# Moving the transposes that close the SSD branch's gated norm into the following weight unit

## The chip, the cores and the metric

The kernel runs on one core of a Trainium2 chip, as one launch. The metric is device time in microseconds, median over several executions. A second number is the time of the one execution that the hardware profiler recorded; all rows below are from that execution.

## The reference, cut to what matters

A decoder trunk of two layers over 256 tokens, width 1024, float32. In each layer one projection feeds three mixers (sliding-window attention A, block attention B, a Mamba-2 SSD branch C), whose outputs are gated and merged; cross-attention and an MLP follow. The part that the change touches is the end of branch C and what reads it:

```python
y = ssd_scan(xh, dt, a, bm, cm) + xh * d_skip[:, None]
y = y.reshape(B, S, SSD_D_INNER) * silu(z)
yg = y.reshape(B, S, SSD_GROUPS, SSD_D_INNER // SSD_GROUPS)        # 2 groups of 512 columns
yg = yg * rsqrt(mean(yg * yg, axis=-1, keepdims=True) + NORM_EPS)
y_c = yg.reshape(B, S, SSD_D_INNER) * ssd_norm
...
merged = g_a * (y_a @ w_br_swa) + g_b * (y_b @ w_br_moba) + g_c * (y_c @ w_br_ssd)
```

## The kernel before, in words

**Weight units.** All dense products of a layer are cut into 93 units, `UNITS[0]` to `UNITS[92]`, each with 1 MB of weights or less, in a ring of three buffers (`RING = 3`). For each unit SyncE's queue (SP) issues the load into `raw` (L606), ScalarE (ACT) rounds it to `w_hi` (`hi`, L721), VectorE (DVE) makes the remainder `w_lo` (`lo`, L1344), and TensorE (PE) multiplies: three products for each tile pair (hi by hi, hi by lo, lo by hi; L1041 to L1043), 48 matmuls of 256 columns in each unit that matters here. Every engine walks the same list of units, written out by hand, in program order; what an engine does in its turn for unit `u` is called slot `u`. In slot `u` ACT and DVE prepare unit `u + 3`, since that buffer is free once unit `u` is done. So in ACT's slot `u` stand, in this order: the closing work of the slot, the evacuation of unit `u`, `hi(u + 3)`, and the exponentials of a job. DVE's slot: the mask of a job, the closing work, the evacuation, `lo(u + 3)`.

**Units around the change.** 27 to 30 are gate columns of branch B, 31 and 32 are `branch_b` (y_b times its weights), 33 to 36 gate columns of branch C, 37 to 40 `branch_c` (y_c times `w_br_ssd`), 41 to 44 the mixing product.

**Small work between units.** Attention and SSD work is placed behind units: 24 jobs (numbers 16 to 23 are the SSD's, at slots 25 to 32), each with a mask on DVE (L1573), an exponential on ACT (L834), a weighting on GpSimd (POOL, L670), and "values" on PE two slots later (`job_values`, eight small matmuls, L1147). SP's queue carries a broadcast of 256 KB for each SSD job (L591) ahead of a weight load; that of job 23 and behind it the load of unit 34 wait for the mask of job 21 (`decays_made`), made in slot 30.

**Closings.** `CLOSINGS` 4 to 7 are the four blocks (128 tokens by 512 columns) of branch C. Closing `i` is at slot `CLOSE_SLOT[i]`: 28, 30, 32, 34. There DVE makes `y_tok` (`close`, L1630 and L1632), ACT squares it with a sum (`close_square`, L858), POOL turns the sum to a reciprocal root in three small operations (L693 to L696), and ACT scales `y_tok` (`close_scale`, L851), at the head of ACT's next slot. Then PE transposes the block (`close_turn`, four 128 by 128 transposes, L1168, into the PSUM bank 7), ACT copies the result times a gain as `yc_hi` (`close_hi_part`, L873, four operations), and DVE makes the remainder `yc_lo` and frees the bank (`close_lo_part`, L1647, four operations). For closings 6 and 7, PE first computes a term "yoff" (two passes at L1233, right behind units 32 and 34) into the same bank 7, so that it waits for the release of that bank. Unit 37 waits for the release of closing 7's bank (`operand_ready`): only then y_c is complete.

**Before the change** all three steps of closing `i` are in slot `CLOSE_SLOT[i] + 1`: PE transposes behind units 29, 31, 33 and 35 (and behind the values of that slot).

Of the kernel before, what the change touches and what calls it, by code (L numbers as in the profile page):

```python
# [134 lines left out]
UNITS = make_units()  # L135
# [12 lines left out]
U_GATE, U_BRA, U_BRB, U_BRC, U_MIX = (first_of(k) for k in ("gate", "branch_a", "branch_b", "branch_c", "mix"))  # L148
# [8 lines left out]
def job_slot(n):  # L157

    return JOB_SLOT0 + n + (SSD_PAUSE if n >= SSD_JOB0 else 0)


def job_at(s):

    return next((n for n in range(NJOBS) if job_slot(n) == s), -1)
# [19 lines left out]
def head_of(j, i):  # L184
# [6 lines left out]
CLOSINGS = [(3, 0, 0, 0), (7, 0, 1, 0), (11, 1, 0, 0), (15, 1, 1, 0),  # L191
            (17, 2, 0, 0), (19, 2, 0, 1), (21, 2, 1, 0), (23, 2, 1, 1)]
CLOSE_SLOT = [job_slot(c[0]) + 2 for c in CLOSINGS]


SB_, TB_, OB_, YB_ = 4, 5, 6, 7
# [11 lines left out]
def slot_banks(s):  # L208

    out = []  # L210
    if s == SWA_T_SLOT:
        out += [(b, ("qkT", i)) for i, b in enumerate((SB_, TB_, OB_))]
    if 0 <= job_at(s) < SSD_JOB0:
        out.append((SB_, ("score", job_at(s))))
    if 0 <= job_at(s - 1) < SSD_JOB0:
        out.append((TB_, ("probsT", job_at(s - 1))))
    if job_at(s - 2) in [0, 4, 8, 12, 16, 18, 20, 22]:
        out.append((OB_, ("values", job_at(s - 2))))
    if s == ACS_SLOT:
        out.append((YB_, ("acs",)))  # L220
    if s == CB_SLOT:
        out.append((YB_, ("cb",)))
    if s == BTOK_SLOT:
        out.append((YB_, ("btok",)))
    if s in XS_SLOTS:
        out += [(YB_, ("xs", XS_SLOTS.index(s), 0)), (SB_, ("xs", XS_SLOTS.index(s), 1))]
    if s == STATES_SLOT:
        out += [(YB_, ("states", 0)), (SB_, ("states", 1))]
    for i, (_, branch, tile, group) in enumerate(CLOSINGS):
        if branch == 2 and tile == 1 and s == CLOSE_SLOT[i]:  # L230
            out.append((YB_, ("yoff", group)))
    for i in range(8):
        if s == CLOSE_SLOT[i] + 1:
            out.append((YB_, ("closeT", i)))
    for n in (1, 2):
        if s == NORM_TURN_SLOT[n]:
            out += [(SB_ + b, ("norm", n, b)) for b in range(4)]
    if s in (U_CO + 2, U_CO + 3):
        out += [(SB_ + b, ("norm", 3, b)) for b in ((0, 1), (2, 3))[s - U_CO - 2]]
    h = s - CROSS_SLOT0  # L240
    if 0 <= h < X_HEADS:
        out.append((SB_, ("xscore", h)))
    if 0 <= h - 1 < X_HEADS:
        out.append((TB_, ("xprobsT", h - 1)))
    if s == U_VX + 2:
        out += [(OB_, ("xvalues", 0)), (YB_, ("xvalues", 1))]
    if s == U_VX + 3:
        out += [(OB_, ("xvalues", 2)), (YB_, ("xvalues", 3))]
    return out
# [58 lines left out]
def trunk(nc, a, out):  # L308
    ctx = ExitStack()
    with ctx:  # L310
# [173 lines left out]
        def bank(key):  # L484
            return psum[:, BANK_OF[key][0], :]
# [223 lines left out]
        def _(act):  # L709
# [186 lines left out]
            for l in range(DEPTH):  # L896
# [20 lines left out]
                for u, w in enumerate(UNITS):  # L917
                    h = u - CROSS_SLOT0
                    for i in range(4, 8):
                        if u == CLOSE_SLOT[i] + 1:  # L920
                            close_scale(l, i)
                    if u == SWA_T_SLOT:
                        for i in range(3):
                            act.wait_ge(*is_full(l, ("qkT", i)))
                            out_of_bank(l, ("qkT", i), qkT_a[:, 2 * i:2 * i + 2, :], two(bank(("qkT", i))))
                    turned_probs(l, job_at(u - 1))
                    if u == CB_SLOT:
                        act.wait_ge(*is_full(l, ("cb",)))
                        out_of_bank(l, ("cb",), cbT[:].rearrange("p k n -> p (k n)"))
                    if u == BTOK_SLOT:  # L930
                        act.wait_ge(*is_full(l, ("btok",)))
                        out_of_bank(l, ("btok",), b_tok[:].rearrange("p k n -> p (k n)"), bank(("btok",))[:, 0:SEQ])
                    if u == STATES_SLOT:
                        for g in range(SSD_GROUPS):
                            act.wait_ge(*is_full(l, ("states", g)))
                            out_of_bank(l, ("states", g), states[:, g, :])
                    for i in range(8):
                        if u == CLOSE_SLOT[i] + 1:
                            close_hi_part(l, i)
                    if 0 <= h - 1 < X_HEADS:  # L940
                        act.wait_ge(*is_full(l, ("xprobsT", h - 1)))
                        out_of_bank(l, ("xprobsT", h - 1), pT_x[:, h - 1, :, :], two(bank(("xprobsT", h - 1))))
                    if w["kind"] == "xbc":
                        hi(l, u + RING)
                    if u in (U_CO + 2, U_CO + 3):
                        norm_gain_hi(l, 3, ((0, 1), (2, 3))[u - U_CO - 2])
                    evacuate(l, u)
                    if w["kind"] == "branch_c":
                        merged_hi(l, w["index"])
                    if u + RING < NU and w["kind"] != "xbc":  # L950
                        hi(l, u + RING)
                    if u == U_SWA:
                        act.wait_ge(*sp_arg.at(l, 1))
                        act.activation(sp[:, 1, :], sp[:, 0, :], ACT.Exp, scale=-1.0).then_inc(sp_exp.sem, 1)
                        act.activation(par[:, PC_EXPA:PC_DSKIP], cols[:, l, PC_EXPA:PC_DSKIP], ACT.Exp)\
                           .then_inc(a_exp.sem, 1)
                    if u == ACS_SLOT:
                        act.wait_ge(*decay_arg.at(l, 1))
                        act.activation(decay[:], decay[:], ACT.Exp).then_inc(decay_exp.sem, 1)
                    for i in range(4, 8):  # L960
                        if u == CLOSE_SLOT[i]:
                            close_square(l, i)
                    exps(l, job_at(u))
                    if 0 <= h < X_HEADS:
                        cross_exps(l, h)
                    for hh in {U_VX + 2: (0, 1), U_VX + 3: (2, 3)}.get(u, ()):
                        cross_out_hi(l, hh)
                    if u == MEM_SQUARE_SLOT:
                        act.wait_ge(*mem_loaded.at(l, 16))
                        act.wait_ge(*ssd_sq.at(l, 4))  # L970
                        for t in range(TT):
                            square(1, t, mem_sb, sq_done.sem)
                    for n in (1, 2):
                        if u == NORM_TURN_SLOT[n]:
                            norm_gain_hi(l, n)
                    if u == NORM_TURN_SLOT[2] or u == U_CO + 3:
                        for t in range(TT):
                            square(2 if u < U_CO else 3, t, x_sb, sq_done.sem)
# [5 lines left out]
        def _(pe):  # L984
# [30 lines left out]
            def unit(l, u, tiles=range(TT)):  # L1015
# [18 lines left out]
                if w["orient"] == "A":  # L1034
                    for m in range(n // P):
                        dst = bank(unit_banks(u, w)[m // 2])[:, (m % 2) * SEQ:(m % 2 + 1) * SEQ]
                        for k in range(kt):
                            if turned and m == 0 and k % 2 == 0:
                                pe.wait_ge(*is_read(l, ("norm", turned, k // 2)))
                            cs = slice(m * P, (m + 1) * P)  # L1040
                            pe.matmul(dst, m_hi[:, k, cs], a_hi[:, k, :], start=k == 0, stop=False)  # L1041
                            pe.matmul(dst, m_hi[:, k, cs], a_lo[:, k, :], start=False, stop=False)  # L1042
                            ins = pe.matmul(dst, m_lo[:, k, cs], a_hi[:, k, :], start=False, stop=k == kt - 1)  # L1043
# [160 lines left out]
            for l in range(DEPTH):  # L1204
                for u in range(NU):
# [43 lines left out]
                    if u == CB_SLOT:  # L1249
                        pe.wait_ge(*xbc_ready.at(l, 6))  # L1250
                        pe.wait_ge(*is_free(l, ("cb",)))
                        for c in range(TT):
                            for g in range(SSD_GROUPS):
                                i = SSD_GROUPS * c + g
# [24 lines left out]
                            pe.matmul(bank(key), b_tok[:, g, :], xdec[:, 512 * g:512 * (g + 1)],  # L1279
                                      start=True, stop=True).then_inc(full(key), 1)  # L1280
                    for i in range(8):
                        if u == CLOSE_SLOT[i] + 1:
                            close_turn(l, i)
                    if 0 <= h < X_HEADS:
                        cross_scores(l, h)
# [9 lines left out]
        def _(dve):  # L1295
# [382 lines left out]
            for l in range(DEPTH):  # L1678
# [7 lines left out]
                lo(l, 2)  # L1686
                for u, w in enumerate(UNITS):
                    h = u - CROSS_SLOT0
                    if 0 <= job_at(u):
                        job_mask(l, job_at(u))  # L1690
                    if u == ACS_SLOT:
# [3 lines left out]
                    if u in XS_SLOTS:  # L1695
                        xs_tokens(l, XS_SLOTS.index(u))
                    for i in range(8):
                        if u == CLOSE_SLOT[i] + 1:
                            close_lo_part(l, i)
                    for i in range(8):  # L1700
                        if u == CLOSE_SLOT[i]:
# [21 lines left out]
                    if 0 <= h < X_HEADS:  # L1723
                        dve.wait_ge(*is_read(l, ("xscore", h)))
                        steps.link(dve.reciprocal(row_max[:], xden[:]))
                        for t in range(TT):
                            s = s_sb[:, h % 2, t * SEQ:(t + 1) * SEQ]
# [43 lines left out]
```

## Time and profile before

| | us |
|---|---|
| median of 3 runs | 1233.14 (1230.57 to 1234.44) |
| profiled execution, its own time | 1229.25 |
| its span, first to last instruction | 1227.5 |
| PE busy | 1183.4 |
| DVE busy | 741.4 |
| ACT busy | 587.4 |
| POOL busy | 87.3 |

The engines' busy times overlap. In the page and the rows, "L1168" is line 1168 of the kernel; `PEld` is the loading of the stationary operand, which overlaps with matmuls. The mean granted clock of TensorE over the execution is 0.997 of full speed. The core's DMA engines move 163 GB/s on average.

### The profile page before, as it was taken

How to read it: one execution, taken by the hardware profiler on the slowest of the kernel's cores; microseconds unless marked ns; L12 is line 12 of the kernel's file. 1: busy time of each engine (PE TensorE's matmuls, PEld its weight loads, DVE VectorE, ACT ScalarE, POOL GpSimd, SP SyncE). 2: the span in 40 equal slices, each digit the busy share in tenths (PEclk: the TensorE clock that was granted, in tenths of full speed). 3: DMA queues.
4: the chain of work that ended last, by engine and by line, in shares of the span. 5: the costliest groups of instructions: out<-in, count | busy, mean ns of one | idle time of the engine just before them, and what ended most of it. 6: DMA issues, size and time to landing. Idle time of an engine off the chain costs nothing.

```text
span 1227.5 us, 19222 instructions
## 1 busy us (share of the span) xinstructions
PE 1183.4 (96%) x8014; PEld 1085.5 (88%) x8014; DVE 741.4 (60%) x1080; ACT 587.4 (48%) x800; POOL 87.3 (7%) x119
## 2 busy tenths in 40 slices
PE   2999999999999999999989999999999999999997
PEld 1998899999898899999879888999999978999996
DVE  3776766685745465555458767568675544645554
ACT  4544544545454354444445554445554444544442
POOL 4000001420000000000020000023100000000000
PEclk9999999999999999999999999999999999999999
DMA  6652534547654446555627444266556453555561
GB/s 154 202 167 75 181 123 140 174 150 258 192 167 133 144 158 200 183 196 171 206 84 228 137 138 135 81 180 217 179 180 198 138 171 104 205 187 191 182 211 38
DMA packets 155424, 201.37 MB, mean 164 GB/s; under 512 B 6097, under 2 KB 110921, under 8 KB 155337
## 3 DMA queue, kind: packets, MB, share of 16 engines
q1 hardware_dynamic: 155208, 200.08, 50.1%
q8 instruction: 64, 1.05, 0.4%
q0 software_dynamic: 128, 0.06, 0.3%
q14 instruction: 24, 0.19, 0.1%
HBM read 199.04 MB, written 1.08 MB: 163 GB/s over the span
## 4 chain that ended last, share of the span: by engine, by line
PE 87%; DVE 4%; ACT 3%; issue 2%; POOL 2%; DMA 2%; SPq 1%; DVEq 0%; POOLq 0%; ACTq 0%
PE psum L1041 15%; PE psum L1042 15%; PE psum L1043 15%; PE psum L1050 10%; PE psum L1052 10%; PE psum L1051 10%; PE psum L1114 2%; PE psum L1155 2%; PE psum L1127 1%; PE psum L1200 1%; PE psum L1177 1%; DMA raw<-in_w_br_moba_dram 1%; PE psum L1085 1%; POOL sms L693 1%; DVE w_lo L1344 1%
## 5 line engine op out<-in xcount | busy, mean ns | idle before, releaser
L1344 DVE TENSOR_TENSOR w_lo<-raw,w_hi 128x2048 fp32r<-128x2048 f32 (+1 forms) x184 | 418.7, 2278 | 267.4 <-ACT w_hi L721 267.4
L721 ACT ACTIVATE w_hi<-raw 128x2048 fp32r<-128x2048 f32 (+2 forms) x188 | 349.2, 1858 | 153.6 <-PE psum L1052 130.9
L1041 PE MATMUL psum<-act_hi,w_hi 128*128 128x256 f32 x1344 | 385.3, 287 | 0.0
L1043 PE MATMUL psum<-act_hi,w_lo 128*128 128x256 f32 x1344 | 380.1, 283 | 0.0
L1042 PE MATMUL psum<-act_lo,w_hi 128*128 128x256 f32 x1344 | 380.1, 283 | 0.0
L1041 PEld LDWEIGHTS psum<-act_hi,w_hi 128*128 128x128 f32 x1344 | 257.6, 192 | 1.9 <-issue 0.5
L1042 PEld LDWEIGHTS psum<-act_lo,w_hi 128*128 128x128 f32 x1344 | 257.7, 192 | 1.1 <-issue 0.5
L1043 PEld LDWEIGHTS psum<-act_hi,w_lo 128*128 128x128 f32 x1344 | 257.5, 192 | 0.0
L1050 PE MATMUL psum<-w_hi,relu_hi 128*128 128x512 f32 x256 | 99.8, 390 | 0.0
L1051 PE MATMUL psum<-w_lo,relu_hi 128*128 128x512 f32 x256 | 99.8, 390 | 0.0
L1052 PE MATMUL psum<-w_hi,relu_lo 128*128 128x512 f32 x256 | 99.6, 389 | 0.0
L1050 PE MATMUL psum<-w_hi,act_hi 128*128 128x512 f32 (+1 forms) x224 | 87.2, 389 | 4.4 <-issue 4.4
L1051 PE MATMUL psum<-w_lo,act_hi 128*128 128x512 f32 (+1 forms) x224 | 85.2, 380 | 0.0
L1052 PE MATMUL psum<-w_hi,act_lo 128*128 128x512 f32 (+1 forms) x224 | 85.2, 380 | 0.0
L777 ACT ACTIVATE tmp<-psum 128x512 f32<-128x512 f32 x32 | 19.1, 597 | 96.0 <-PE psum L1043 96.0
L756 ACT ACTIVATE pT_sb<-psum 128x256 f32<-128x256 f32 (+1 forms) x32 | 15.7, 490 | 96.1 <-PE psum L1127 96.1
L658 POOL TENSOR_TENSOR ms<-sq,pool_c 128x1 f32<-128x1 f32 (+1 forms) x12 | 9.1, 759 | 693.9 <-ACT tmp L728 642.4
L1052 PEld LDWEIGHTS psum<-w_hi,relu_lo 128*128 128x128 f32 x256 | 48.1, 188 | 10.1
L1050 PEld LDWEIGHTS psum<-w_hi,relu_hi 128*128 128x128 f32 x256 | 48.1, 188 | 9.5
L1051 PEld LDWEIGHTS psum<-w_lo,relu_hi 128*128 128x128 f32 x256 | 48.1, 188 | 9.5
L1050 PEld LDWEIGHTS psum<-w_hi,act_hi 128*128 128x128 f32 x224 | 42.8, 191 | 12.5 <-issue 5.4
L1052 PEld LDWEIGHTS psum<-w_hi,act_lo 128*128 128x128 f32 x224 | 42.8, 191 | 8.2
(245 smaller groups left out, 1788.9 us busy)
## 6 DMA issues: line engine op xcount, KB each, us to landing
raw<-in_w_in_dram SPq DMA_DIRECT2D x36, 1024.0 KB, 5.2
raw<-in_w_up_dram SPq DMA_DIRECT2D x32, 1024.0 KB, 5.4
raw<-in_w_down_dram SPq DMA_DIRECT2D x32, 1024.0 KB, 5.1
raw<-in_w_gate_dram SPq DMA_DIRECT2D x24, 1024.0 KB, 7.1
raw<-in_w_ckv_dram SPq DMA_DIRECT2D x16, 1024.0 KB, 5.3
raw<-in_w_br_ssd_dram SPq DMA_DIRECT2D x8, 1024.0 KB, 9.6
raw<-in_w_mix_out_dram SPq DMA_DIRECT2D x8, 1024.0 KB, 5.1
raw<-in_w_cq_dram SPq DMA_DIRECT2D x8, 1024.0 KB, 5.1
```

The costliest lines, as they stand in the source:

```text
L721: ins = act.activation(w_hi[:, slot, cut], raw[:, slot, cut], ACT.Copy)
L756: act.activation(dst, src, ACT.Copy).then_inc(free(key), 1)
L777: act.activation(tmp[:, j % 2, :], bank((u, 0)), ACT.Relu).then_inc(free((u, 0)), 1)
L1041: pe.matmul(dst, m_hi[:, k, cs], a_hi[:, k, :], start=k == 0, stop=False)
L1042: pe.matmul(dst, m_hi[:, k, cs], a_lo[:, k, :], start=False, stop=False)
L1043: ins = pe.matmul(dst, m_lo[:, k, cs], a_hi[:, k, :], start=False, stop=k == kt - 1)
L1050: pe.matmul(dst, a_hi[:, k0 + k, ts], m_hi[:, k, :], start=first, stop=False)
L1051: pe.matmul(dst, a_hi[:, k0 + k, ts], m_lo[:, k, :], start=False, stop=False)
L1052: ins = pe.matmul(dst, a_lo[:, k0 + k, ts], m_hi[:, k, :], start=False, stop=last)
L1114: ins = pe.matmul(bank(key)[:, i * 2 * P:i * 2 * P + (t + 1) * P], qk[half_p, q_tile, t * P:(t + 1) * P], qk[half_p, k_tile, 0:(t + 1) * P ...
L1155: ins = pe.matmul(bank(key)[:, hs], pT_sb[:, n % 2, c:c + P], v, start=k == 0, stop=k == t)
L1344: dve.tensor_tensor(w_lo[:, slot, 0:n], raw[:, slot, 0:n], w_hi[:, slot, 0:n].bitcast(F32), ALU.subtract).then_inc(lo_ready.sem, 1)
```

## The change

The transposes of closings 4 to 7 move one slot on, into the inside of a unit. For closings 0 to 3 nothing changes. `INNER_TURN` is {30: (4, (1, 0)), 32: (5, (1, 0)), 34: (6, (1, 0)), 36: (7, (0, 4))}: inside unit 30, closing 4's transposes stand ahead of column tile m = 1, inner tile k = 0, and so on. Units 30, 34 and 36 have two column tiles of eight inner tiles, so (1, 0) is behind 24 of the 48 matmuls and (0, 4) behind 12; unit 32 has four column tiles of four inner tiles, so (1, 0) is behind 12. ACT's `close_hi_part` and DVE's `close_lo_part` move on to slots 30, 32, 34 and 36 too, and DVE's stands at the head of its slot, ahead of the mask. `close_scale`, `close_square` and `close` stay. In bank 7 the order of use stays closing 5, yoff, closing 6, yoff, closing 7.

```diff
--- before.py
+++ after.py
@@ -191,6 +191,9 @@
 CLOSINGS = [(3, 0, 0, 0), (7, 0, 1, 0), (11, 1, 0, 0), (15, 1, 1, 0),
             (17, 2, 0, 0), (19, 2, 0, 1), (21, 2, 1, 0), (23, 2, 1, 1)]
 CLOSE_SLOT = [job_slot(c[0]) + 2 for c in CLOSINGS]
+TURN_SLOT = [CLOSE_SLOT[i] + (1 if c[1] < 2 else 2) for i, c in enumerate(CLOSINGS)]
+INNER_TURN = {TURN_SLOT[i]: (i, (0, 4) if i == 7 else (1, 0)) for i, c in enumerate(CLOSINGS) if c[1] == 2}
+assert all(UNITS[u]["orient"] == "A" and u < U_BRC for u in INNER_TURN)
 
 
 SB_, TB_, OB_, YB_ = 4, 5, 6, 7
@@ -226,12 +229,12 @@
         out += [(YB_, ("xs", XS_SLOTS.index(s), 0)), (SB_, ("xs", XS_SLOTS.index(s), 1))]
     if s == STATES_SLOT:
         out += [(YB_, ("states", 0)), (SB_, ("states", 1))]
+    for i in range(8):
+        if s == TURN_SLOT[i]:
+            out.append((YB_, ("closeT", i)))
     for i, (_, branch, tile, group) in enumerate(CLOSINGS):
         if branch == 2 and tile == 1 and s == CLOSE_SLOT[i]:
             out.append((YB_, ("yoff", group)))
-    for i in range(8):
-        if s == CLOSE_SLOT[i] + 1:
-            out.append((YB_, ("closeT", i)))
     for n in (1, 2):
         if s == NORM_TURN_SLOT[n]:
             out += [(SB_ + b, ("norm", n, b)) for b in range(4)]
@@ -935,7 +938,7 @@
                             act.wait_ge(*is_full(l, ("states", g)))
                             out_of_bank(l, ("states", g), states[:, g, :])
                     for i in range(8):
-                        if u == CLOSE_SLOT[i] + 1:
+                        if u == TURN_SLOT[i]:
                             close_hi_part(l, i)
                     if 0 <= h - 1 < X_HEADS:
                         act.wait_ge(*is_full(l, ("xprobsT", h - 1)))
@@ -1035,6 +1038,8 @@
                     for m in range(n // P):
                         dst = bank(unit_banks(u, w)[m // 2])[:, (m % 2) * SEQ:(m % 2 + 1) * SEQ]
                         for k in range(kt):
+                            if u in INNER_TURN and INNER_TURN[u][1] == (m, k):
+                                close_turn(l, INNER_TURN[u][0])
                             if turned and m == 0 and k % 2 == 0:
                                 pe.wait_ge(*is_read(l, ("norm", turned, k // 2)))
                             cs = slice(m * P, (m + 1) * P)
@@ -1279,7 +1284,7 @@
                             pe.matmul(bank(key), b_tok[:, g, :], xdec[:, 512 * g:512 * (g + 1)],
                                       start=True, stop=True).then_inc(full(key), 1)
                     for i in range(8):
-                        if u == CLOSE_SLOT[i] + 1:
+                        if u == TURN_SLOT[i] and u not in INNER_TURN:
                             close_turn(l, i)
                     if 0 <= h < X_HEADS:
                         cross_scores(l, h)
@@ -1686,6 +1691,8 @@
                 lo(l, 2)
                 for u, w in enumerate(UNITS):
                     h = u - CROSS_SLOT0
+                    if u in INNER_TURN:
+                        close_lo_part(l, INNER_TURN[u][0])
                     if 0 <= job_at(u):
                         job_mask(l, job_at(u))
                     if u == ACS_SLOT:
@@ -1695,7 +1702,7 @@
                     if u in XS_SLOTS:
                         xs_tokens(l, XS_SLOTS.index(u))
                     for i in range(8):
-                        if u == CLOSE_SLOT[i] + 1:
+                        if u == TURN_SLOT[i] and u not in INNER_TURN:
                             close_lo_part(l, i)
                     for i in range(8):
                         if u == CLOSE_SLOT[i]:
```

## Rows read from the trace of the kernel before

**Rows 1.** Page, part 4: shares of the span on the chain that ended last.
```profile
PE 87%; DVE 4%; ACT 3%; issue 2%; POOL 2%; DMA 2%; SPq 1%; DVEq 0%; POOLq 0%; ACTq 0%
```

**Rows 2.** Waits of PE: line, releaser, us in total, times, longest.
```profile
PE psum L1168 <- ACT y_tok L851: 5.1, 7, 1.3
```

**Rows 3.** Timeline of PE, layer 0: start, duration, line, operands, count [idle before].
```profile
231.10 1.00 PE L1147 MATMUL psum<-xdt,s_sb 128*128 128x64 f32 x8
232.95 0.66 PE L1168 MATMUL psum<-ident,y_tok 128*128 128x128 f32 x4 [0.85 <-ACT y_tok L851]
233.36 0.36 PE L1041 MATMUL psum<-act_hi,w_hi 128*128 128x256 f32 x1
...
245.84 1.00 PE L1147 MATMUL psum<-xdt,s_sb 128*128 128x64 f32 x8
247.00 0.66 PE L1168 MATMUL psum<-ident,y_tok 128*128 128x128 f32 x4 [0.15 <-ACT y_tok L851]
...
253.24 1.02 PE L1233 MATMUL psum<-states,xbcT 128*128 128x512 f32 x2
254.10 1.00 PE L1147 MATMUL psum<-xdt,s_sb 128*128 128x64 f32 x8
254.91 0.36 PE L1041 MATMUL psum<-act_hi,w_hi 128*128 128x256 f32 x1
...
260.74 1.00 PE L1147 MATMUL psum<-xdt,s_sb 128*128 128x64 f32 x8
262.83 0.66 PE L1168 MATMUL psum<-ident,y_tok 128*128 128x128 f32 x4 [1.09 <-ACT y_tok L851]
...
276.45 0.28 PE L1043 MATMUL psum<-act_hi,w_lo 128*128 128x256 f32 x1
277.03 0.66 PE L1168 MATMUL psum<-ident,y_tok 128*128 128x128 f32 x4 [0.30 <-ACT y_tok L851]
...
283.27 0.28 PE L1041 MATMUL psum<-yc_hi,w_hi 128*128 128x256 f32 x1
```

**Rows 4.** Timeline of PE, layer 1: closing 4.
```profile
832.52 0.66 PE L1168 MATMUL psum<-ident,y_tok 128*128 128x128 f32 x4 [1.29 <-ACT y_tok L851]
```

**Rows 5.** Timeline of ACT, layer 0: `hi(34)`, closing 7's `yc_hi`, `hi(38)`.
```profile
249.59 1.92 ACT L721 ACTIVATE w_hi<-raw 128x2048 fp32r<-128x2048 f32 x1 [0.76 <-DMA raw<-in_w_gate_dram]
...
277.72 1.14 ACT L873 ACTIVATE yc_hi<-psum,par 128x128 fp32r<-128x128 f32 x4 [0.75 <-PE psum L1168]
...
281.11 1.91 ACT L721 ACTIVATE w_hi<-raw 128x2048 fp32r<-128x2048 f32 x1 [1.51 <-DMA raw<-in_w_br_ssd_dram]
```

**Rows 6.** Timeline of DVE, layer 0: masks 21 and 23, an evacuation, `lo(35)`, `yc_lo`, `lo(38)`.
```profile
240.31 1.41 DVE L1573 SCALAR_TENSOR_TENSOR s_sb<-pT_sb,acs,mask_ssd 128x128 f32<-128x128 f32 x4 [0.67 <-PE psum L1147]
...
255.84 1.13 DVE L1573 SCALAR_TENSOR_TENSOR s_sb<-pT_sb,acs,mask_ssd 128x128 f32<-128x128 f32 x4
...
261.00 0.68 DVE L1526 SCALAR_TENSOR_TENSOR tmp<-g_sb,psum 128x512 f32<-128x512 f32 x1
...
262.32 3.36 DVE L1344 TENSOR_TENSOR w_lo<-raw,w_hi 128x2048 fp32r<-128x2048 f32 x1
...
278.90 1.13 DVE L1647 SCALAR_TENSOR_TENSOR yc_lo<-psum,par,yc_hi 128x128 fp32r<-128x128 f32 x4 [3.62 <-ACT yc_hi L873]
283.05 2.29 DVE L1344 TENSOR_TENSOR w_lo<-raw,w_hi 128x2048 fp32r<-128x2048 f32 x1 [3.02 <-ACT w_hi L721]
```

**Rows 7.** Timeline of POOL, layer 0: a small operation of closing 6, weighting of job 23.
```profile
261.21 0.19 POOL L694 TENSOR_TENSOR sms<-sms,pool_c 128x1 f32<-128x1 f32 x1
...
261.99 1.54 POOL L670 TENSOR_TENSOR s_sb<-s_sb,cbT 128x512 f32<-128x512 f32 x1
```

**Rows 8.** Timeline of SP's queue, layer 0: broadcast for job 23, load 34 behind it.
```profile
241.74 0.34 SPq L591 DMA_DIRECT2D pT_sb<-acs_rows  x1
```

**Rows 9.** Timeline of PE at the layers' border, and its clock there.
```profile
624.52 0.47 PE L1050 MATMUL psum<-w_hi,act_hi 128*128 128x512 f32 x1 [2.78 <-issue]
```

**Rows 10.** Windows: length, busy us of PE, PEld, DVE, ACT, POOL, granted clock, DMA.
```profile
625.40:628.40 3.00, 3.00 (x9) 2.32 (x8) 2.48 (x3) 0.16 (x2) 2.61 (x3) 0.50 0.20 68
```

## The prediction

> **What bounds the kernel now.** I read the chain of waits first: PE holds 87% of it, DVE, ACT and POOL together 9% [rows 1]. So time comes and goes where PE stands still. The table of PE's waits says for what: at the closings' transposes it waits 5.1 us in 7 pieces for ACT's scaled `y_tok` [rows 2]. PE has no wait between the last of them in a layer and the end of `branch_c`, so whatever is lost or won at the closings goes straight to the end. Third, the timelines of PE, ACT, DVE, POOL and SP side by side through one layer's closings: there one sees what is ready when the transposes come half a unit later.
>
> **What is removed.** Eight values take 0.81 us up to the next instruction (254.10 to 254.91 in [rows 3]). PE would be free for the transposes at 231.91, 246.65, 261.55 and, one matmul of 0.12 behind 276.45, at 276.57; they start at 232.95, 247.00, 262.83 and 277.03 [rows 3]. That is 1.04 + 0.35 + 1.28 + 0.46 = 3.13 us in layer 0. In layer 1 the idle time before closing 4 is 1.29 instead of 0.85 [rows 3, 4], so 3.57. Inside a unit the four transposes still take 0.41 (232.95 to 233.36), and the first matmul behind them is 0.36 long instead of 0.28 [rows 3]: one more such switch than before, 0.09 each, 0.36 in a layer. If nothing else waited, the gain would be 2.8 + 3.2 = 6.0 us. The new places are late enough for `y_tok`: by the same rows (its transposes started as soon as it was there) it is ready just before 232.95, 247.00 and 262.83, and PE would come by at 231.91 + 0.08 + 24 x 0.12 = 234.9, about 247.2 and about 264.5. Only closing 5 is tight (0.1 to 0.4 us).
>
> **What is moved, and what stands ahead of it.** `yc_hi` and `yc_lo` now stand in the next slot of ACT and DVE, so behind `hi(u)` and `lo(u)` of a unit three ahead of the slot they left: closing 4 behind hi and lo of unit 32, closing 5 of unit 34, closing 6 of 36, closing 7 of 38. In each of these slots the weights must have landed before the closing can be read. Someone waits for that reading: nobody for closing 4; for closing 5 and 6 the yoff pass behind units 32 and 34 (same bank); for closing 7 unit 37.
>
> *Closing 4.* Its transposes are over at 235.4, ACT and DVE read it by about 239.2. DVE's mask 21 waits for the values behind unit 30 anyway, which come at 238.25 instead of 239.20; a mask starts 1.11 behind them (240.31 - 239.20). So mask 21 is not delayed, and 0.95 us of the gain is kept up to here. It ends at 240.5 instead of 241.7: the start is earlier by 0.95 and it is 1.14 long instead of 1.41, since POOL has finished. SP waits for it with the broadcast of job 23 and load 34 [rows 8], so these go out 1.2 us earlier.
>
> *Closing 5.* `hi(34)` starts when load 34 lands, at 249.59 [rows 5]; 1.2 earlier is 248.4. It takes 1.95 to DVE's start (281.11 to 283.05 for unit 38 [rows 5, 6]), so `lo(34)` runs from 250.35 for 2.2 (2.29, of which the next instruction overlaps 0.1), and `yc_lo` from 252.6 for 1.13 [rows 6]: bank 7 is free at 253.75. PE wants it for yoff at 246.65 - 0.95 + 0.08 + 5.76 + 0.5 = 252.05. So yoff starts at about 253.8 instead of 253.24 [rows 3]: the lead of 1.2 us that PE had has become a lag of 0.56. Both ends: if load 34 lands no earlier, because the transfer and not its issue sets it, 1.2 more; if it lands early enough for `lo(34)` to be done by 251, nothing is lost (lag -1.2). POOL's weighting of job 22 runs just then. `lo(35)` beside the weighting of job 23 took 3.36 instead of 2.29 [rows 6, 7]; if `yc_lo` were held up the same way, 1.1 more. I take none: POOL's L694 ran at 261.21 for 0.19 inside DVE's L1526, which reads PSUM and one tile of SBUF as `yc_lo` does [rows 6, 7]. The Trainium skill ("SBUF — State Buffer", Who interferes with whom) says that a DVE instruction with two SBUF inputs locks out a GpSimd one that reads SBUF and the reverse, whichever is first, and one with a single SBUF input does not; the trace agrees on both, 3.36 beside 2.29 and 0.19 undisturbed. By the rule applied to `lo(34)`, which starts before that weighting, POOL waits and not DVE.
>
> *Closing 6.* Mask 23 was held by DVE itself (255.84 [rows 6]); now it waits for values 21, 0.86 + 1.11 behind yoff: 255.8, the same. `lo(35)` ends at 265.6, `lo(36)` follows until 267.8, `yc_lo` until 268.85, while PE, 0.56 late, wants yoff at 261.55 + 0.56 + 5.84 (the unit) + 0.5 (the transposes) = 268.45. A stall of 0.5; the lag falls from 0.56 to about -0.1.
>
> *Closing 7.* Here is the largest term. SP holds load 38 behind the memory's load, and that behind the last `y_tok` (closing 7), so `hi(38)` waits for DMA and starts at 281.11 [rows 5], and `lo(38)` at 283.05 [rows 6]. Both move with PE's lag only (-0.1). Before, `yc_hi` (277.72) and `yc_lo` (278.90) ran in the 3 us in which ACT and DVE were waiting for this load. Now `yc_hi` comes at 282.9 and `yc_lo` behind `lo(38)`: 282.95 + 2.2 = 285.2, plus 1.13, plus 0.1 to PE: unit 37 starts at 286.4. PE would have been ready at 276.57 - 0.1 + 0.08 + 5.76 + 0.5 = 282.8. It stands 3.6 us still, and unit 37 starts 3.15 later than at 283.27 [rows 3]. Layer 1 is the same with numbers 0.2 to 0.4 smaller (mask 21 gains 1.65 instead of 1.2): about +2.9. Nothing gives it back: units 37 to 44 are PE bound, and their loads are ahead.
>
> **The clock.** A pause of 2.78 us at the layers' border is followed, some 0.8 us after PE's restart, by 3 us at a granted clock of 0.50, the 1.2 GHz level [rows 9, 10]; PE then does the work of 1.5 us in 3. No other pause behind full work is that long now, and there will be two more (3.6 and 3.3 us). I take one of the two to fall: +1.5. Both ends: none (0) and both (+3). The Trainium skill ("TensorE: Matmul & The Clock Gate", What's actually happening) says that the engine is throttled by default and that its recent activity alone releases it, with a moment of change that differs from run to run; by it a fall is possible at both pauses in any run, which would make the sum 9.1. The trace agrees that a pause is enough (2.78 us), and with one pause it can't say how sure a fall is.
>
> **Sum.** 3.15 + 2.9 + 1.5 = 7.5 us on the profiled execution's own 1229.25: 1236.8. The median of the runs is 3.9 above that execution, and the difference is added to it: 1233.14 + 7.5 = 1240.6.
>
> **Rivals.**
> - *Only unit 37 stalls* (load 34 lands early enough, yoff finds bank 7 free). Then per layer -1.2 - 1.2 + 3.2 and -1.6 - 1.2 + 3.2: +1.2 in all, 1234.3, or 1235.8 to 1237.3 with the clock. For it: DMA is half idle around 241. Against: `hi(34)` waited 0.76 for its load already. 12%.
> - *The reading of closing 7 is hidden*, the change does what its gaps promise: -6.0, 1227.1. One mechanism: load 38 lands by 278, ahead of the transposes. From a landing of 280.0 or earlier the change is faster. Against: `hi(38)` waited 1.51 us for it [rows 5], and nothing in the change moves it. 8%.
> - *The clock falls twice in both layers' stalls*: 3.15 + 2.9 + 3.0 = +9.1, 1242.2. 23%; and no fall at all, +6.0, 1239.2, 20%.
> - *yc_lo(5) is blocked by POOL or load 34 keeps its landing*: 1.1 us more in each layer, of which closing 6 gives back nothing: +9.7, 1242.8. 10%.
> The forecast with one fall has 27%.
>
> About 0.3% (3.7 us) is what a measurement of this kernel can tell from no change; so slower means above 1236.8. The forecast, the clock's two cases and the blocked bank are slower (27 + 23 + 20 + 10 = 80%), less 2 for stalls overrated by a microsecond each. Same holds most of the first rival and these 2, 13%; faster the second and a little of the first, 9%. The range that leaves out 2 in 10 goes from 1234.5 to 1243.5; among the slower cases alone it is 1238.5 to 1243.
>
> **What would show it.** In PE's waits, L1168 nearly vanishes; new are waits for DVE's `yc_lo` (L1647) of 1.5 to 2 us ahead of L1233 behind unit 32, about 0.5 behind unit 34, and 3 to 3.6 us ahead of the first matmul of unit 37, in both layers. On DVE's timeline `yc_lo` follows `lo(34)`, `lo(36)` and `lo(38)` without a pause. SP's broadcast of job 23 goes out about 1.2 us earlier against the values of job 18. The window of 3 us behind unit 37's start shows 0.50 or 1.00. Wrong would be: `yc_lo` of closing 7 ahead of `lo(38)`, or `hi(38)` not waiting for DMA.

## The result, and the profile after

The changed kernel takes 1239.43 us (median of 6, 1238.86 to 1240.78), the kernel before in the same rounds 1231.28 (6 runs, 1229.07 to 1234.44). The ratio is 1.0068, with an interval from 1.0056 to 1.0080: slower by 8.4 us (6.9 to 9.9) by the ratio, 8.2 by the medians. Forecast were +7.5 us and a time of 1240.6, range 1234.5 to 1243.5.

The profiled execution after took 1240.78 with a span of 1239.0: 11.5 us over the span before, so this pair of traces shows 3 us more than the medians. Where these 3 come from is said below, as far as it is known.

PE's waits after, the rows that answer to [rows 2] (line numbers moved by 5; columns: line, releaser, us in total, times, longest):

```profile
PE psum L1046 <- issue: 7.6, 2, 4.1
...
PE psum L1238 <- DVE yc_lo L1652: 2.8, 4, 1.1
...
PE psum L1173 <- ACT y_tok L854: 1.2, 2, 0.6
```

The old wait is down from 5.1 to 1.2 us; in its place stand 2.8 us ahead of yoff, in four pieces, and 7.6 in two. These two are the first matmuls of unit 37 in either layer. The page calls them "issue", for want of an event it could tie them to; that it is the wait for closing 7 is read from DVE's timeline, where `yc_lo` ends just before. PE, layer 0, answers to [rows 3]:

```profile
234.76 0.60 PE L1173 MATMUL psum<-ident,y_tok 128*128 128x128 f32 x4
...
238.07 1.00 PE L1152 MATMUL psum<-xdt,s_sb 128*128 128x64 f32 x8
...
247.81 0.66 PE L1173 MATMUL psum<-ident,y_tok 128*128 128x128 f32 x4 [0.60 <-ACT y_tok L854]
...
253.54 1.13 PE L1238 MATMUL psum<-states,xbcT 128*128 128x512 f32 x2 [0.78 <-DVE yc_lo L1652]
...
264.92 0.60 PE L1173 MATMUL psum<-ident,y_tok 128*128 128x128 f32 x4
...
268.87 1.10 PE L1238 MATMUL psum<-states,xbcT 128*128 128x512 f32 x2 [0.49 <-DVE yc_lo L1652]
...
277.89 0.60 PE L1173 MATMUL psum<-ident,y_tok 128*128 128x128 f32 x4
...
282.52 0.28 PE L1048 MATMUL psum<-act_hi,w_lo 128*128 128x256 f32 x1
286.34 0.55 PE L1046 MATMUL psum<-yc_hi,w_hi 128*128 128x256 f32 x1 [3.54 <-issue]
286.69 0.41 PE L1047 MATMUL psum<-yc_lo,w_hi 128*128 128x256 f32 x1
```

The transposes of closing 7 are over at 278.5, and unit 37 starts at 286.34. What lies between is on ACT and DVE. First ACT, then DVE, answering to [rows 5] and [rows 6]:

```profile
248.21 1.92 ACT L724 ACTIVATE w_hi<-raw 128x2048 fp32r<-128x2048 f32 x1 [0.46 <-DMA raw<-in_w_gate_dram]
...
280.96 1.91 ACT L724 ACTIVATE w_hi<-raw 128x2048 fp32r<-128x2048 f32 x1 [3.38 <-DMA raw<-in_w_br_ssd_dram]
282.78 1.13 ACT L876 ACTIVATE yc_hi<-psum,par 128x128 fp32r<-128x128 f32 x4
```

```profile
239.18 1.14 DVE L1578 SCALAR_TENSOR_TENSOR s_sb<-pT_sb,acs,mask_ssd 128x128 f32<-128x128 f32 x4
...
250.16 2.29 DVE L1349 TENSOR_TENSOR w_lo<-raw,w_hi 128x2048 fp32r<-128x2048 f32 x1
252.37 1.12 DVE L1652 SCALAR_TENSOR_TENSOR yc_lo<-psum,par,yc_hi 128x128 fp32r<-128x128 f32 x4
...
282.91 2.29 DVE L1349 TENSOR_TENSOR w_lo<-raw,w_hi 128x2048 fp32r<-128x2048 f32 x1 [7.76 <-ACT w_hi L724]
285.12 1.12 DVE L1652 SCALAR_TENSOR_TENSOR yc_lo<-psum,par,yc_hi 128x128 fp32r<-128x128 f32 x4
```

ACT stands idle for 3.38 us in front of `hi(38)`; the transposes of closing 7, which stands behind it, are in the bank for the last 2.5 of these. DVE is idle for 7.76. `yc_hi` and `yc_lo` then follow without a pause.

The granted clock fell inside both pauses, before PE started again, and was still low behind them. Windows (length; busy us of PE, PEld, DVE, ACT, POOL; granted clock; DMA share; GB/s):

```profile
285.00:286.00 1.00, 0.00 (x0) 0.00 (x0) 1.00 (x5) 0.62 (x1) 0.00 (x0) 0.93 1.10 349
286.30:289.30 3.00, 2.96 (x14) 2.99 (x15) 1.97 (x1) 0.99 (x1) 0.00 (x0) 0.50 0.85 314
...
890.00:891.00 1.00, 0.00 (x0) 0.00 (x0) 1.00 (x1) 0.67 (x3) 0.00 (x0) 0.51 1.10 347
892.00:895.00 3.00, 2.77 (x13) 2.80 (x14) 2.33 (x2) 0.77 (x1) 0.00 (x0) 0.50 0.88 285
895.00:898.00 3.00, 3.00 (x20) 3.00 (x20) 0.10 (x1) 0.00 (x0) 0.00 (x0) 0.69 0.71 220
```

Matching PE's instructions of the two traces one by one gives the lag of the changed kernel along the way: -0.1 us at the start, +3.1 at the first matmul of unit 37, +4.4 some 3 us later, +5.8 behind the layers' border, +9.4 at unit 37 of layer 1, +11.5 some 4 us later, and no more up to the end. So 3.2 and 3.6 us are the stalls net of the gain, 1.3 and 2.1 the two falls of the clock, and 1.4 arose at the border, where no instruction was changed. There the pause of 2.78 us of [rows 9] is 2.79 long after the change and full clock follows it; PE waits 2.57 instead of 0.98 for the second tile, and the clock falls at the end of that wait instead:

```profile
634.52 1.97 PE L1071 MATMUL psum<-ident,h_tok 128*128 128x128 f32 x8 [2.57 <-ACT h_tok L908]
```

In both traces these transposes wait for ACT and start the same time behind PE's restart (630.07 - 624.52 = 5.55 us before, 634.52 - 628.98 = 5.54 after). So before the change the slow matmuls of the first tile only shortened the wait and cost nothing; after it the fall met the transposes, 1.97 us long instead of 1.09, and the matmuls behind them. The ten traces of this document all have this pause (2.78 to 2.80 us) and these 5.5 us, and a fall on one side of the wait: in five ahead of it (before, closing 7 alone, closing 7 later, early reading, load 38 early), in five at its end (the changed kernel, closing 7 back, the filler, the last two). The side does not go with what the kernels do at the closings, so I count these 1.4 as scatter between executions. The rest of the 3 us fits the place of the two executions in their series: the one before is near its lowest run, the one after is its highest.

### The profile page after: what moved, and what is told of

Its sections match the earlier page's. It is cut to its first block, busy times and chain, and to the rows that moved or that the text cites. A ratio compares the mean times of both kernels' runs of the same rounds, so it can differ in the third digit from the quotient of the medians.

```text
span 1239.0 us, 19222 instructions
## 1 busy us (share of the span) xinstructions
PE 1187.8 (96%) x8014; PEld 1089.6 (88%) x8014; DVE 738.1 (60%) x1080; ACT 586.7 (47%) x800; POOL 90.5 (7%) x119
## 3 DMA queue, kind: packets, MB, share of 16 engines
HBM read 199.04 MB, written 1.08 MB: 162 GB/s over the span
## 4 chain that ended last, share of the span: by engine, by line
PE 84%; DVE 5%; DMA 4%; ACT 3%; issue 2%; POOL 1%; SPq 1%; DVEq 0%; POOLq 0%; ACTq 0%
PE psum L1046 14%; PE psum L1047 14%; PE psum L1048 14%; PE psum L1055 10%; PE psum L1057 10%; PE psum L1056 10%; DVE w_lo L1349 2%; PE psum L1119 2%; PE psum L1160 2%; ACT w_hi L724 1%; DMA raw<-in_w_br_ssd_dram 1%; PE psum L1132 1%; DMA raw<-in_w_gate_dram 1%; PE psum L1205 1%; DMA raw<-in_w_br_moba_dram 1%
```

## The experiments

Times are medians; each ratio is to the kernel before, in the same rounds of five.

**Closing 7 back, closings 4 to 6 moved**

```diff
-TURN_SLOT = [CLOSE_SLOT[i] + (1 if c[1] < 2 else 2) for i, c in enumerate(CLOSINGS)]
-INNER_TURN = {TURN_SLOT[i]: (i, (0, 4) if i == 7 else (1, 0)) for i, c in ... if c[1] == 2}
+TURN_SLOT = [CLOSE_SLOT[i] + (2 if i in (4, 5, 6) else 1) for i, c in enumerate(CLOSINGS)]
+INNER_TURN = {TURN_SLOT[i]: (i, (1, 0)) for i in (4, 5, 6)}
```

> Closings 4, 5 and 6 as in the changed kernel, closing 7 back behind unit 35. Theory (unit 37 waits because closing 7 is read behind hi(38) and lo(38)): the pause ahead of unit 37 is gone and with it the clock's fall there; what is left is the net of closings 4 to 6, -0.1 us in layer 0 and -0.4 in layer 1: before - 0.5 us (-1.5 to +0.7). PE's waits show yoff waiting 2.5 to 3 us in all. Rival (the loss is spread over all four closings, each transposition inside a unit costing PE and its neighbours): three quarters of the loss stay, before + 6.

1229.31 us, ratio 0.9992 (0.9981 to 1.0003): no difference from before, and the loss is gone. Its profile has no wait ahead of unit 37; yoff waits 3.4 us in all, a little more than the 2.5 to 3 expected:

```profile
PE psum L1238 <- DVE yc_lo L1652: 3.4, 4, 1.6
PE psum L1173 <- ACT y_tok L854: 2.0, 4, 0.7
```

**Only closing 7 moved**

```diff
-TURN_SLOT = [CLOSE_SLOT[i] + (1 if c[1] < 2 else 2) for i, c in enumerate(CLOSINGS)]
-INNER_TURN = {TURN_SLOT[i]: (i, (0, 4) if i == 7 else (1, 0)) for i, c in ... if c[1] == 2}
+TURN_SLOT = [CLOSE_SLOT[i] + (2 if i == 7 else 1) for i, c in enumerate(CLOSINGS)]
+INNER_TURN = {TURN_SLOT[7]: (7, (0, 4))}
```

> Only closing 7 is moved, closings 4 to 6 stand as before the change. Theory: unit 37 starts about 3.2 us late in each layer, and the clock falls behind each of the two pauses at 1.3 us each: before + 9 us (+6.4 without a fall, +9.5 with both long). That is at least the whole loss of the changed kernel. Rival (spread over all four): a quarter of it, before + 2.

1240.61 us, ratio 1.0080 (1.0066 to 1.0095), 9.8 us by the ratio, just over the 9.5 expected with both falls long. PE waits ahead of unit 37 in both layers, 3.5 and 3.7 us:

```profile
PE psum L1046 <- issue: 7.2, 2, 3.7
```

One closing carries the whole loss. The other three seem to bring back about 1 us (the run above is 1.0 below before by its ratio, this one 1.4 above the changed kernel), but no interval here tells that from nothing. The rival of an even spread falls with both runs.

**The reading of closings 5 to 7 ahead of the next unit's weights**

```diff
@@ ACT, and the same on DVE with close_lo_part @@
-                        if u == TURN_SLOT[i]:
+                        if u == TURN_SLOT[i] and i not in (5, 6, 7):
                             close_hi_part(l, i)
...
                     evacuate(l, u)
+                    for i in (5, 6, 7):
+                        if u == TURN_SLOT[i] - 1:
+                            close_hi_part(l, i)
...
                     if u + RING < NU and w["kind"] != "xbc":
                         hi(l, u + RING)
```

> All transposes stay inside their units as in the changed kernel; only ACT's copy and DVE's remainder of closings 5, 6 and 7 move ahead of hi and lo of units 34, 36 and 38, at the end of the slot before. Theory (the order on ACT's and DVE's queues is the cause, not the place on PE): no wait ahead of yoff and unit 37, the gain of the gaps comes out: before - 5.5 us (-4.5 to -6.5). Rival (the place on PE is the cause: the transposes are simply too late for their readers): closing 7's reading would still end about 281.5, no gain beyond before - 2, or a loss where ACT, now waiting for PE inside the slot, delays hi(38): before + 2.

1225.37 us, ratio 0.9959 (0.9946 to 0.9971), 5.4 us below before by the medians. PE's transposes stand where the change put them; only the queues of ACT and DVE differ from it, and 13 to 14 us lie between the two kernels (0.9959 against 1.0068; they ran in different rounds, so the ratios to the kernel before are what compares them). Among PE's waits there is none for `yc_lo` and none ahead of unit 37; for the scaled `y_tok` it still waits 1.9 us (first line). Then ACT, layer 0:

```profile
PE psum L1176 <- ACT y_tok L854: 1.9, 4, 0.8
...
277.04 1.14 ACT L876 ACTIVATE yc_hi<-psum,par 128x128 fp32r<-128x128 f32 x4
280.38 1.92 ACT L724 ACTIVATE w_hi<-raw 128x2048 fp32r<-128x2048 f32 x1 [2.19 <-DMA raw<-in_w_br_ssd_dram]
```

`hi(38)` waits for its load as before, but `yc_hi` no longer stands behind it.

**Load 38 ahead of the memory's load**

```diff
-                    if u == U_BRC + 1:
+                    if u == U_BRC + 2:
                         sp.wait_ge(*ssd_y.at(l, 4))
                         sp.dma_start(mem_sb[:], ...)
```

> The changed kernel with one line of SP's queue moved: load 38 goes ahead of the memory's load and no longer waits for the last y_tok. Theory (what keeps closing 7 waiting is hi(38), and that is the transfer): hi(38) starts right behind the evacuation of unit 35, about 277.5, the remainder of closing 7 is ready at about 282.8, the pause ahead of unit 37 shrinks from 3.5 to 0.2 us and the clock stays up: before - 0.5 us (-1.5 to +1). Rival (the pause is the order of the slots whatever the load, ACT and DVE being too slow to do both): at least half of it stays, before + 4 or more.

1229.37 us, ratio 0.9993 (0.9983 to 1.0004). The order of ACT and DVE is that of the changed kernel; only the load is early (issued at 265.01, ahead of the last `y_tok` and of the memory's load; which of the two had held it up is not told apart). ACT, then PE's wait for yoff:

```profile
276.97 1.91 ACT L724 ACTIVATE w_hi<-raw 128x2048 fp32r<-128x2048 f32 x1
278.77 1.14 ACT L876 ACTIVATE yc_hi<-psum,par 128x128 fp32r<-128x128 f32 x4
...
PE psum L1238 <- DVE yc_lo L1652: 3.5, 3, 2.2
```

PE has no wait to speak of ahead of unit 37 in either layer (in layer 0 its first matmul starts 0.32 us behind the last of unit 36 instead of 0.12). The waits ahead of yoff stay, and so the gain of the gaps does not come out as it did in the run above. So the loss takes both: a reading behind `hi(38)`, and a load 38 that lands late. Either taken away, it goes.

**Closing 7's transposes still later** (only the piece of the line that differs is shown)

```diff
-(0, 4) if i == 7
+(1, 4) if i == 7
```

> The changed kernel with closing 7's transposes another 24 matmuls (2.9 us) later inside unit 36. Theory (ACT's hi(38) and DVE's lo(38) set the time, PE's place does not): the transposes, from 280.8, are still over before ACT comes to them at 282.8; same as the changed kernel, before + 8 (+7 to +9.5). Rival (how late the transposes are on PE sets the pause): 2.9 us more in each layer, before + 14.

1240.25 us, ratio 1.0075 (1.0058 to 1.0091): that of the changed kernel, within the intervals. The pauses ahead of unit 37 are no longer either, 3.5 and 3.6 us:

```profile
PE psum L1046 <- issue: 7.1, 2, 3.6
```

Between these two places inside unit 36, PE's place has no part in the pause.

**PE kept busy through the pause**

```diff
                 wait_lo(pe, l, u)
+                if u == U_BRC:
+                    pe.wait_ge(*is_free(l, (u, 0)))
+                    f_hi = w_hi[:, slot, 0:kt * n].rearrange("p (k n) -> p k n", n=n)
+                    for r in range(28):
+                        pe.matmul(bank((u, 0))[:, 0:SEQ], f_hi[:, r % 8, 0:P], act_hi[:, r % 8, :],
+                                  start=True, stop=True)
                 operand_ready(l, u)
```

> The changed kernel with 28 more matmuls of 256 columns on PE, into unit 37's own bank, ahead of its wait for closing 7 (3.4 us of work in a pause of 3.5 and 4.1 us; the results are overwritten). Theory (the pauses cost twice, once as they are and once because the clock falls to 1.2 GHz behind them, 1.3 us in layer 0 and 2.0 in layer 1): the pause is filled, unit 37 runs at full clock, the changed kernel - 3 us, before + 5 (+4 to +6). Rival (the fall costs nothing that shows in the time, or it has another cause than the pause): same as the changed kernel, before + 8.

1237.44 us, ratio 1.0048 (1.0033 to 1.0063): 6.6 us over before by the medians, 5.9 by the ratio, where 5 was expected. The clock stays at 1.00 behind both pauses:

```profile
282.50:286.00 3.50, 3.50 (x30) 3.36 (x28) 2.84 (x4) 2.68 (x8) 0.00 (x0) 1.00 1.10 346
286.00:289.00 3.00, 2.53 (x21) 2.46 (x21) 1.84 (x3) 1.61 (x1) 0.00 (x0) 1.00 0.74 253
...
892.00:895.00 3.00, 3.00 (x28) 3.00 (x27) 2.25 (x1) 0.00 (x0) 0.00 (x0) 1.00 0.83 320
```

and what is left of the wait is named for what it is:

```profile
PE psum L1052 <- DVE yc_lo L1658: 0.7, 2, 0.5
```

More work on PE made the kernel faster. The changed kernel itself did not run in these rounds, but the kernel with closing 7 still later, which has the same pauses, did: 1240.25 against 1237.44, 2.8 us, and the slowest run with the filler (1238.70) is below the fastest without (1238.81). So the theory's 3 us for the clock stand; what was too low is the rest, 5.9 to 6.6 in place of 5, at or over the upper end of the range.

**Early reading, and closing 5 twelve matmuls later in its unit** (again the piece of the line alone)

```diff
-(i, (0, 4) if i == 7 else (1, 0))
+(i, {5: (2, 0), 7: (0, 4)}.get(i, (1, 0)))
```

> The kernel with early reading of closings 5, 6 and 7 (e3_read_early), and closing 5's transposes 12 matmuls later in unit 32 (behind 24 of 48). There PE waited 0.8 and 0.6 us for the scaled y_tok. Theory (that wait is only the place being 1.4 us too early): it goes, the reading is still over before yoff wants the bank: before - 6.6 us (-5.8 to -7.2). Rival (what PE gains there it gives back at yoff, since ACT now stands in front of hi(34) until the transposes come, and lo(34) and its followers move): same as e3_read_early, before - 5.4.

1224.32 us, ratio 0.9942 (0.9927 to 0.9958), 6.5 us below before by the medians. The transposes of closing 5 start without a wait at 248.73, and yoff too:

```profile
248.73 0.60 PE L1176 MATMUL psum<-ident,y_tok 128*128 128x128 f32 x4
...
252.04 1.02 PE L1241 MATMUL psum<-states,xbcT 128*128 128x512 f32 x2
```

Against the kernel without this step (0.9959) the intervals overlap; the profile shows the wait gone, the times alone don't prove the 1 us.

**All three**, the last kernel with load 38 early as well:

> e7_early_and_five_later with load 38 ahead of the memory's load as well. Theory: with closing 7 read ahead of hi(38), that transfer keeps nobody waiting any more, so the earlier load brings nothing: same as e7_early_and_five_later within 0.7 us, before - 6.6. Rival (hi(38), hi(39) and hi(40) behind it still hold back branch_c or the mixing product): up to 1 us better, before - 7.6.

1223.62 us, ratio 0.9938 (0.9923 to 0.9952). The load's part can't be told from nothing, and its rival is not ruled out either (7.2 us by the medians lies between 6.6 and 7.6). This is the lowest median, 0.6% below before and 1.3% below the changed kernel: the idea of the change was sound, with the readers moved along the other way.

## Why the prediction was right, point by point

- **The gap's gain** (6.0 us if nothing else waited): the kernels with early reading bring 5.4 and 6.5, near what was worked out, though the first still waits 1.9 us for `y_tok`.
- **Closing 4 and mask 21**: values behind unit 30 were forecast at 238.25, and came at 238.07 in a trace that runs 0.1 ahead; mask 21 starts at 239.18 (239.36 forecast), and is 1.14 long. The broadcast behind it went out at 240.35 instead of 241.74 [rows 8], 1.3 us earlier.
- **Closing 5**: `hi(34)` 248.21 (248.4), `lo(34)` 250.16 (250.35), `yc_lo` 252.37 (252.6), yoff 253.54 (253.8). Neither bound came in: load 34 did land earlier, and `yc_lo` took 1.12 although POOL's weighting of job 22 was running (250.72 for 2.87). What the prediction had wrong is that `y_tok` of closing 5 would be ready when it was before: it came at 247.81 instead of 247.00, and PE stood 0.60 us still for it. POOL's first small operation started at 244.41 and was not over until `lo(33)` was, as before; but `lo(33)` itself was 0.8 later, since `hi(33)` had waited for load 33 until 241.81 instead of 240.90. The load was issued at the same time (234.70 and 234.72); why it landed later is not shown, but `hi(33)` waits 2.7 to 3.2 us for it in layer 0 of every trace in which closing 4 is moved, and 0.67 before. This wait cost nothing here, since `yc_lo` set yoff, but it took the place of a part of yoff's: that was forecast at 1.5 to 2 us behind unit 32, and is 0.78 in layer 0 and 1.08 in layer 1. It is the tight place (0.1 to 0.4 us) of the prediction, on its wrong side.
- **Closing 6**: a stall of 0.5, measured 0.49 in both layers.
- **Closing 7**: a pause of 3.6 and a start at 286.4, measured 3.54 and 286.34. In layer 1 I had put the net at +2.9; it is +3.6, with a pause of 4.08. There load 38 landed 0.4 us later after its issue than in layer 0 or before (`hi(38)` 8.5 us behind the memory's load, against 8.0 to 8.1). That is this execution's: the traces with closing 7 alone and with closing 7 later have 7.9 to 8.2 and pauses of 3.7 and 3.6 in layer 1.
- **The clock** is the term that was mis-sized: one fall of 1.5 us was assumed, the even choice between none and two. In the profiled execution both came, and cost 1.3 and 2.1. Two falls are also the rule. The traces of the three kernels with the pauses (the changed one, closing 7 alone, closing 7 later) have a fall in or just behind each of the six pauses, the trace with the filler at neither place. And the mean granted clock was 0.993 in four of the changed kernel's six runs and 0.994 and 0.996 in the others, against 0.996 or 0.997 in 21 of 23 runs of the kernel before and 0.996 to 0.998 in all six with the filler; 0.003 of 1239 us is 3.7. So the rival with two falls (+9.1) described what happens, not the forecast of one.
- **The sum**: that +7.5 lies so near the measured 8.2 is in part luck. The terms as this pair of traces has them make 3.2 + 3.6 + 1.3 + 2.1 = 10.2; with a pause of 3.6 or 3.7 in layer 1, as in the other two kernels, it would be some 0.4 less, near the 9.5 and 9.8 by which these two lie above before. Why the changed kernel's own median lies lower isn't settled; its interval reaches to 9.9. The forecast of the time itself, 1240.6, rests on a median before of 1233.14 from three runs; six runs made it 1231.28, and this error of 1.9 us went against the one in the sum.
- **The rivals**: "only unit 37 stalls" was wrong in its premise (yoff waits 2.8 us), and "the reading is hidden" became true only when load 38 or the order was changed. Its turning point, a landing of 280.0, does not follow from the prediction's own terms. From the start of `hi(38)` to that of unit 37 they give 1.95 + 2.2 + 1.13 + 0.1 = 5.4 us, so that unit 37 keeps its old start of 283.27 only if `hi(38)` starts by 277.9; from 280.0 it would start at 285.4, 2.1 us late. The run with load 38 early (`hi(38)` at 276.97, no wait ahead of unit 37) agrees with 277.9; nothing between 277 and 281 was tried.

## What to carry to other kernels

When a step is moved into a later slot, its readers on other in-order engines move with it: list what each of those queues holds ahead of it there, and look at the transfer that the first of them waits for. Idle time of 3 us on ACT and DVE looked like room; it was the wait of an instruction that would now stand in front. Here a reader that someone waits for belonged ahead of the preparation of a unit that is three units away.

## What the runs showed of the hardware

Pauses of the same length at the same place, the 2.8 us at the layers' border, had different sequels: in five of the ten traces the granted clock was down when PE restarted or fell soon after (0.8 us after the restart in the trace before), in the other five it stayed up until the end of the next wait. Pauses of 3.5 to 4.1 us behind full work had a fall each of the six times that a trace shows one, and cost 1.3 us (3 us at 0.50) and 2.1 us in the changed kernel. Shorter waits can have one too: with load 38 early, yoff waits 2.24 us in layer 1 and the clock is down before it starts, and with closing 7 alone it is down 0.8 us behind a wait of 1.47 us in layer 0, while the wait of 1.29 us at the same step in layer 1 of the trace before had no fall.

```profile
852.55 2.07 PE L1238 MATMUL psum<-states,xbcT 128*128 128x512 f32 x2 [2.24 <-DVE yc_lo L1652]
853.00:854.00 1.00, 1.00 (x2) 0.39 (x2) 0.00 (x0) 0.00 (x0) 0.00 (x0) 0.50 0.97 321
...
235.13 0.65 PE L1173 MATMUL psum<-ident,y_tok 128*128 128x128 f32 x4 [1.47 <-ACT y_tok L854]
236.00:239.00 3.00, 3.00 (x16) 3.00 (x15) 1.13 (x4) 3.00 (x7) 0.00 (x0) 0.50 0.38 113
```

The clock can be low already when PE restarts (286.34: the matmuls behind the first are 0.21 apart instead of 0.12) or fall within a microsecond of it (closing 7 alone, both layers). The Trainium skill ("TensorE: Matmul & The Clock Gate", What's actually happening) says that the moment at which the clock is released varies from run to run; these traces show the same of the moment at which it falls.
